# The adding DMAs read their second operand from SBUF, and the fills are put into a new order

## What is computed

```python
def swiglu_ffn(x, w_gate_up, w_down):
    g, u = jnp.split(x @ w_gate_up, 2, axis=-1)
    return (jax.nn.silu(g) * u) @ w_down

for layer in range(DEPTH):                       # DEPTH = 2, D_FF = 2816
    x = x + 0.5 * swiglu_ffn(rms_norm(x, ffn1_norm[layer]), ...)
    x = x + mixer(rms_norm(x, mix_norm[layer]))  # layer 0: windowed GQA, layer 1: latent attention
    x = x + 0.5 * swiglu_ffn(rms_norm(x, ffn2_norm[layer]), ...)
return rms_norm(x, final_norm)
```

## Time and profile before

| | us |
|---|---|
| runs (3) | 1857.53 median, 1855.23 to 1859.74 |
| profiled execution, its time | 1855.27 |
| profiled execution, span from first to last instruction | 1853.5 |
| PE busy in the span | 1737.3 |
| DVE busy | 1417.2 |
| ACT busy | 954.8 |
| POOL busy | 434.8 |
| mean granted TensorE clock | 0.981 |

### The profile page before, as it was taken

One profiled execution on the slowest core, in us unless ns is written; L12 is line 12 of the kernel. 1 busy time (PEld: TensorE's weight loads), 2 busy tenths in 40 slices (PEclk: granted clock), 3 DMA queues, 4 the chain that ended last, 5 costly groups with the idle time before them and its releaser, 6 DMA issues. The chain is left out here.

```text
span 1853.5 us, 34651 instructions
## 1 busy us (share of the span) xinstructions
PE 1737.3 (94%) x12937; PEld 1626.4 (88%) x12937; DVE 1417.2 (76%) x2776; ACT 954.8 (52%) x1892; POOL 434.8 (23%) x495
## 2 busy tenths in 40 slices
PE   5999999999989999999799999999999889999997
PEld 4999999877879899998799999987867789999995
DVE  5788787667678878866778788766897568878788
ACT  4554554446555545544555455544565445555452
POOL 0333333111013333330133333300000033333320
PEclk7999999999989999999899999999999989999999
DMA  5899999533439999995399999945112389999971
GB/s 173 192 219 237 224 220 229 149 110 91 125 91 220 221 228 217 226 245 154 69 224 224 226 223 230 209 117 132 30 40 58 108 182 220 230 226 221 226 163 69
DMA packets 187076, 324.18 MB, mean 175 GB/s; under 512 B 24545, under 2 KB 58526, under 8 KB 186910
## 3 DMA queue, kind: packets, MB, share of 16 engines
q0 software_dynamic: 66816, 121.66, 38.5%
q1 hardware_dynamic: 118528, 198.55, 33.9%
q10 hardware_dynamic: 1566, 1.74, 0.3%
HBM read 315.33 MB, written 2.10 MB: 171 GB/s over the span
## 5 line engine op out<-in xcount | busy, mean ns | idle before, releaser
L1889 PE MATMUL bank<-h_all,w_all 128*128 128x256 f32 x2352 | 672.2, 286 | 45.0 <-ACT work L1042 34.0
L1890 PE MATMUL bank<-h_all,w_all 128*128 128x256 f32 x2352 | 668.2, 284 | 0.0
L1891 PE MATMUL bank<-h_all,w_all 128*128 128x256 f32 x2352 | 668.0, 284 | 0.0
L1889 PEld LDWEIGHTS bank<-h_all,w_all 128*128 128x128 f32 x2352 | 453.9, 193 | 52.4 <-issue 34.4
L1890 PEld LDWEIGHTS bank<-h_all,w_all 128*128 128x128 f32 x2352 | 454.1, 193 | 0.0
L1891 PEld LDWEIGHTS bank<-h_all,w_all 128*128 128x128 f32 x2352 | 453.9, 193 | 0.0
L787 POOL DMA_DIRECT2D work<-ffn_gu x252 | 221.6, 923 | 825.3 <-DVE w_all L1238 593.3
L901 ACT ACTIVATE w_all<-work 128x512 fp32r<-128x512 f32 x352 | 208.9, 623 | 345.6 <-DMA work<-ffn_gu 222.3
L1238 DVE TENSOR_TENSOR w_all<-work,w_all 128x512 fp32r<-128x512 f32 x352 | 238.9, 687 | 150.4 <-ACT w_all L901 149.6
L1238 DVE TENSOR_TENSOR w_all<-r_all,w_all 128x512 fp32r<-128x512 f32 (+1 forms) x356 | 308.2, 866 | 21.7 <-ACT w_all L901 16.9
L901 ACT ACTIVATE w_all<-r_all 128x512 fp32r<-128x512 f32 (+1 forms) x356 | 273.0, 769 | 73.3 <-PE bank L1891 71.9
(11 more groups left out here) (214 smaller groups left out, 2787.1 us busy)
## 6 DMA issues: line engine op xcount, KB each, us to landing
work<-ffn_gu POOLq DMA_DIRECT2D x252, 256.0 KB, 5.9
r_all<-ffn_gu SPq DMA_DIRECT2D x88, 512.0 KB, 5.2
r_all<-ffn_gu SPq DMA_DIRECT2D x172, 256.0 KB, 6.3
work<-ffn_d POOLq DMA_DIRECT2D x96, 256.0 KB, 6.1
work<-ffn_gu SPq DMA_DIRECT2D x88, 256.0 KB, 5.6
r_all<-ffn_gu POOLq DMA_DIRECT2D x84, 256.0 KB, 7.2
r_all<-ffn_d SPq DMA_DIRECT2D x64, 256.0 KB, 5.8
r_all<-ffn_d SPq DMA_DIRECT2D x32, 512.0 KB, 5.3
```

The costliest lines, as they stand in the source:

```text
L1889: t.matmul(o, wh, xh, start=c == 0 and not on, stop=False, skip_group_check=on)
L1890: t.matmul(o, wh, xl, start=False, stop=False, skip_group_check=on)
L1891: last = t.matmul(o, wl, xh, start=False, stop=c == PAIRED - 1, skip_group_check=on)
```

## The change

Three things are changed together.

1. The addend of all adding DMAs (`link` and `join`) is the plain buffer of the unit in SBUF, not HBM. POOL therefore waits for the plain buffer's load before each, and SP waits, before it loads a plain buffer anew, for the third adding DMA of the unit that used it. In the last block the loads of `ffn_rows` wait for the adding DMAs of units 27, 28 and 29.
2. In a unit, FB(u) and FE(u) move from the end of iteration u-1 into iteration u: FB before FU(u+1), FE after the copy s_1. The addition of product 7 moves to the start of the next iteration on DVE (`finish`, `finish_late`). The third link of a unit is issued at the start of its own iteration.
3. At the start of a block: `pairs_out` evacuates a tile before it splits the next weights and fills FA(0), FU(0), FC(0) at j = 4, 5, 6 in place of 6, 7 and the end; FU(1) is filled at its end. In block 0 the combinations of the pairs move behind the sum of squares, and PE does `sums` after the second half of the plain tile and `spread` after product 2.

```diff
     def fill_count(f, kind, u):
-        at = {FA: 0, FU: 1, FC: 2}[kind] if u == 0 else {FU: 3, FA: 4, FB: 5, FE: 6, FC: 9, FD: 11}[kind]
-    elif u == NU - 1 and kind in (FC, FD):
-        at = 6 * NU - (5 if kind == FC else 4)
+        at = {FA: 0, FU: 1, FC: 2}[kind] if u == 0 else {FU: 3, FA: 4, FB: 5, FE: 6, FC: 9, FD: 10}[kind]
+    elif kind in (FU, FA):
+        at = (7 if kind == FU else 8) if u == 2 else 6 * u - (6 if kind == FU else 4)
     else:
-        at = 6 * u + {FU: -5, FA: -4, FB: -2, FE: 0, FC: 3, FD: 5}[kind]
+        at = 6 * u - 1 + {FB: 0, FE: 2, FC: 4, FD: 5}[kind]
...
     def load_plain(f, u):
-                if u >= 3:
-                    sp.wait_ge(fill_lo, fill_count(f, FC, u - 3))
-                elif f > 0:
-                    sp.wait_ge(fill_lo, fill_count(f - 1, FC, u - 3 + NU))
+                if u >= 3 or f > 0:
+                    fe, ue = (f, u - 3) if u >= 3 else (f - 1, u - 3 + NU)
+                    sp.wait_ge(fill_lo, fill_count(fe, FC, ue))
+                    if ue > 0:
+                        sp.wait_ge(chain_sum[(NU * fe + ue) % CHAIN], chain_count(fe, ue, 3))
...
     def load(n, src):
                 if n >= N_LAST and i < SLOTS:
+                    for u in (NU - 3, NU - 2, NU - 1):
+                        sp.wait_ge(chain_sum[(NU * f + u) % CHAIN], chain_count(f, u, 3))
...
     def link(f, u, step):
-                pool.dma_start(chain[g % CHAIN], unit_source(f, u, slice(part * S, (part + 1) * S)), accum_op=ALU.add
+                pool.wait_ge(plain_in[(u + 2) % 3], unit_count(f, u))
+                pool.dma_start(chain[g % CHAIN], plain[(u + 2) % 3][:, part * S:(part + 1) * S], accum_op=ALU.add
...
     def ffn(f, m):                                  # POOL
                 link(f, 1, 0)
                 join(f, 1)
-                for u in range(NU + 1):
+                for u in range(NU):
+                    if u > 0:
+                        link(f, u, 2)
                     link(f, u + 1, 1)
                     if u == 0:
                         power(m)
                     link(f, u + 2, 0)
                     join(f, u + 2)
-                    link(f, u + 1, 2)
...
     def pairs_out(n, f, begun=0):                   # ACT; DVE alike
+                if not begun:
+                    high(n + AHEAD, end)
                 for j in range(KD):
-                    if j >= begun:
-                        high(n + j + AHEAD, end)
-                    if j == KD - 2:
-                        high_fill(f, FA, 0)
-                    if j == KD - 1:
-                        high_fill(f, FU, 0)
+                    high(n + j + AHEAD + 1, end)
+                    if 4 <= j < 7:
+                        high_fill(f, (FA, FU, FC)[j - 4], 0)
+                    if j >= 2 and j % 2 == 0:
+                        high_mixed(h_mix, combine_count(f, j // 2 - 1, False), j // 2 - 1)
...
     def ffn(f):                                     # ACT
+                    if u > 1:
+                        high_fill(f, FB, u)
                     high_fill(f, FU, u + 1)
...
+                    if u > 1:
+                        high_fill(f, FE, u)
                     high_fill(f, FA, u + 1)
...
-                    high_fill(f, FB, u + 1)
+                    if before:
+                        silu(f, u - 1, 1)
                     high_fill(f, FD, u)
...
-                    high_fill(f, FE, u + 1)
...
     def ffn(f, m):                                  # DVE
+                    if u > 1:
+                        finish(f, u - 1)
+                        low_fill(f, FB, u)
                     low_fill(f, FU, u + 1)
+                    if u > 1 and UNITS[u - 1][0] == "D":
+                        finish_late(f, u - 1)
...
     def ffn(f, m, ready):                           # PE
                 plain_tile(f, False)
-                sums(m, KD)
+                if f > 0:
+                    sums(m, KD)
                 plain_tile(f, True)
                 if f > 0:
                     pe.wait_ge(evac_done, ready)
+                else:
+                    sums(m, KD)
                 product(f, 1, 1)
-                spread(m + 1)
-                for q in (2, 6, 5, 7):
+                if f > 0:
+                    spread(m + 1)
+                product(f, 2, 1)
+                if f == 0:
+                    spread(m + 1)
+                for q in (6, 5, 7):
                     product(f, q, 1)
```

More of the change, by code:

```diff
@@ L794, in join @@
                 pool.wait_ge(single_in[u % SINGLE], single_count(f, u))
-                pool.dma_start(single[u % SINGLE], unit_source(f, u, slice(0, S)), accum_op=ALU.add
+                pool.wait_ge(plain_in[(u + 2) % 3], unit_count(f, u))
+                pool.dma_start(single[u % SINGLE], plain[(u + 2) % 3][:, 0:S], accum_op=ALU.add
                                ).then_inc(single_sum[u % SINGLE], 16)
@@ L970, in pairs_out @@
                     squared(xT[:, PERM[j], :], j == 0)
-                    if j % 2 == 0 and j >= 2:
-                        high_mixed(h_mix, combine_count(f, j // 2 - 1, False), j // 2 - 1)
-                high_fill(f, FC, 0)
+                high_fill(f, FU, 1)
             def begin(f):
-                high_fill(f, FU, 1)
+                if f == 0:
+                    high_fill(f, FU, 1)
+                    high_fill(f, FA, 1)
+                    for q in range(PAIRED - 1):
+                        high_mixed(h_mix, combine_count(f, q, False), q)
                 high_mixed(h_mix, combine_count(f, PAIRED - 1, False), PAIRED - 1)
-                high_fill(f, FA, 1)
+                if f > 0:
+                    high_fill(f, FA, 1)
                 high_fill(f, FB, 1)
@@ L1077, in _ @@
                 squared(xT[:, PERM[j], :], j == 0)
-                if j % 2 and j < KD - 1:
-                    high_mixed(h_mix, combine_count(0, j // 2, False), j // 2)
             end = SEG_AT[1]
@@ L1342, in pairs_out @@
                 end = n + KD
+                if not begun:
+                    low(n + AHEAD, end)
                 for j in range(KD):
-                    if j >= begun:
-                        low(n + j + AHEAD, end)
-                    if j == KD - 2:
-                        low_fill(f, FA, 0)
-                    if j == KD - 1:
-                        low_fill(f, FU, 0)
                     b = product(n + j)
@@ L1463, in second_half, with finish, finish_late @@
                 v.tensor_tensor(hid_half(UNITS[u][1], 1), c_22[u % 2], g_1, ALU.mult).then_inc(late_half, 1)
+            def finish(f, u):
+                dve.wait_ge(prod_done, product_count(f, 7, u))
+                if UNITS[u][0] == "G":
+                    dve.wait_ge(e_7, order_of(f, u) + 1)
+                    dve.wait_ge(late_half, TILES * f + max(UNITS[u][1] - 1, 1))
+                    v.tensor_tensor(c_22[u % 2], C_BANKS[u % 2][:, 0:HN], u_3, ALU.add).then_inc(e_5, 1)
+                else:
+                    x_added(UNITS[u][2] + PAIRED, 1, B_BANKS[u % 2][:, 0:HN]).then_inc(e_7, 1)
+            def finish_late(f, u):
+                dve.wait_ge(e_7, order_of(f, u) + 1)
+                x_added(UNITS[u][2] + PAIRED, 1, C_BANKS[u % 2][:, 0:HN]).then_inc(e_5, 1)
             def ffn(f, m):
@@ L1496, in ffn @@
                         x_added(c0, 0, D_BANK[:, 0:HN]).then_inc(e_2, 1)
+                    if u > 1:
+                        low_fill(f, FE, u)
                     low_fill(f, FA, u + 1)
@@ L1536, in ffn @@
                         low(SEG_AT[f] + 1, end)
-                    if gate:
-                        dve.wait_ge(e_7, at + 1)
-                        dve.wait_ge(prod_done, product_count(f, 7, u))
-                        dve.wait_ge(late_half, TILES * f + max(UNITS[u][1] - 1, 1))
-                        v.tensor_tensor(c_22[u % 2], c, u_3, ALU.add).then_inc(e_5, 1)
-                    else:
-                        dve.wait_ge(prod_done, product_count(f, 7, u))
-                        x_added(c1, 1, b).then_inc(e_7, 1)
                     if q is not None:
                         low_mixed(y_mix, k, q % PAIRED)
-                    low_fill(f, FE, u + 1)
-                    if not gate:
-                        dve.wait_ge(e_7, at + 1)
-                        x_added(c1, 1, c).then_inc(e_5, 1)
                     if f == FFNS - 1 and u > DOWN_END[1]:
```

49 lines of the change are left out of this document (30 added, 19 removed).

## The result

The changed kernel takes 1842.12 us (median of 7 runs, 1840.71 to 1847.77) where the kernel before took 1857.53 (7 runs): a ratio of 0.9924, 95% interval 0.9908 to 0.9939, or 15.4 us less. The forecast was 1829.5, 28 us less.

The account below looks back on a forecast made before the run. PE was busy 1737.3 of 1853.5 us, with DVE and the DMA engines near it. Gains of 19 + 5 + 3 + 11 + 5 less losses of 8 and 7 made 28, so a median of 1829.5 us, range 1800 to 1877.

Parts of the forecast that it names:

- two serial reads stay two serial reads: Adding DMAs: taking the addend from SBUF changes nothing in a packet's cost; bounds 0 to 2.2 us a unit.
- rival (c): Adding DMAs with SBUF addends land 1 us or more sooner than 5.9, no ring misses: 1809 us; chance 0.20.
- 19 + 5 - 8 = 16 us: Units: 19 gained at waits for u_3, 5 where D units begin, 8 lost to small misses of the ring.
- the new order takes FB(u+1) from in front of u_3: Combining units: FB's landing gets 3 to 4 us more; 28 us of u_3 waits can go, 19 counted.
- The ring of the plain buffers: Units: link 2, plain load, link 0, FU, link 1, FB take 27.9 of 30.1 us; 8 us lost, bounds 0 to 56.
- 8 waits of 1.42: Where D units begin: PE's waits shrink to 0.8, as low_mixed is drawn forward and FE goes behind; 5 us gained.
- Block 0 was to start product 6(1) at about 51: Start of block 0: DVE's reordered work reaches about 51 before product 6(1) can start; 3 us gained, not 14.65.
- the four starts: Block starts: 3 us from block 0, 0 and 1.5 from blocks 1 and 3, 6 from block 2, 3 from FU(1); 14 together.
- The clock: After PE waits, as at the start of block 1: half of some 10 us of low-clock loss goes, 5 us gained.
- the wait for link 2: End of block 3: ffn_rows loads wait for unit 29's link 2, delaying product 7 by 6.5; 7 us lost with transposes.
- rival (a): Units: waits mostly move; ring misses and DVE lateness take 0.3 us in each of 112 units: 1855 us; chance 0.14.
- the signs that were named: Profile after: u_3 below 18 us, four units 41 or less, adding share near 38%, block 3 wait 5 to 8, acc wait split.

Follow-up runs that it names:

- order_only: Changed kernel with addends read from HBM again and without the waits the SBUF source brought, leaving parts 2 and 3: 1881.37 us, 1.0104 of the kernel before.
- hbm_waits: Changed kernel with its order and new waits kept, but all addends read from HBM again: 1886.68 us, 1.015 of the kernel before.
- fu_behind: Changed kernel with FU(u+1) filled behind the copy s_1 and its addition, on ACT and DVE: 1849.23 us, 0.9944 of the kernel before.
- starts_old: Changed kernel with part 3, the new block starts, taken back on ACT, DVE and PE: 1857.31 us, 0.999 of the kernel before.
- ends_fixed: Changed kernel with SP's table loads behind four down-weight loads and ffn_rows loads waiting only for units whose buffers they overwrite: 1821.31 us, 0.9792 of the kernel before.
- fb_behind_u3: Kernel before plus parts 1 and 3 and the mended ends, with FB(u+1) filled behind copy u_3 and product 7's addition: 1807.11 us, 0.9714 of the kernel before.
- source_only: Kernel before with only part 1, addends from SBUF and the waits that brings: 1843.21 us, 0.9905 of the kernel before.

## Why the prediction came out as it did

**The source of the addend: the step that failed.** The prediction says of it "I take nothing: two serial reads stay two serial reads". The price of a packet did stay, at 0.171 us. But a DMA's price for the engines and its time to land are two things. The landings fell from 5.9 to 5.2 us for the links, and part 1 alone, source and waits together, was worth 16 us. The rival (c) had the right place. Its step of 1 us or more came for the first link in the old order (1.6) and for no other, where it had it for all, on top of an order that was to bring 19 by itself. The Trainium skill's HBM Reference, section Latency, has 2 us for an access at high load; 0.7 us is what the links' landings show in the old order, 0.3 to 0.6 with order and waits equal. By the two rates of the Trainium skill's DMA: Bandwidth & Descriptors, section Where 436 GB/s comes from, the source would not matter; by the packets it didn't, by the time it did.

**The new order: right by the sum, wrong by the cause.** Units were to gain 19 + 5 - 8 = 16 us and gained 16.1. That the two agree is luck: with the old source the same order loses 20.7 there, and with the new source the old order gains 17.7. In the step "the new order takes FB(u+1) from in front of u_3" I followed what FB left and not what it came to stand ahead of. FB at the head of an iteration puts FU(u+1), and with it a landing, in front of s_1 a moment later: ACT stood 13 us for FU's landing in all (units 4 to 28) in the kernel before, 50 in the changed one, 89 in `order_only`. And link 2 goes out behind FB, at 3.3 us into its iteration (median; 1.1 before) where I had 1.7. So the order as a whole gained at product 4 only as far as landings came sooner (30.0 us lost before, 12.2 changed, 27.0 in `order_only`), and lost at product 6 (17.1, 20.7, 34.9). The ring of the plain buffers, priced at 8 us and feared at 56, is not in these losses: `hbm_waits` and `order_only` differ by 2.3 us in the units.

**The D groups.** 8 waits of 1.42 were to shrink to 0.8. Product 6 of the first D units lost 13.0 us before and 11.1 after, 1.39 a time, so 2 us came of the 5. Only `fu_behind` brought it to 0.78.

**The starts held.** Block 0 was to start product 6(1) at about 51; it started at 50.45, behind a wait that is now in two:

```profile
40.21 0.65 PE L2008 MATMUL bank<-ident,st 128*128 128x128 f32 x4 [2.25 <-DVE st L1329]
50.45 0.57 PE L1916 MATMUL bank<-h_all,w_all 128*128 128x256 f32 x1 [9.58 <-DVE w_all L1250]
```

14 us were counted for the four starts, 5.5 + 7.5 = 13.0 measured, and `starts_old` gives 12 to 15. The parts lay otherwise: block 0 gained 5.5 for 3, block 2 7.4, block 3 2.9, and block 1 lost 2.8. Its stage holds the low clock behind the end of block 0, and in `ends_fixed`, without that, it is 2.0 us shorter than before.

**The clock: a term that didn't come.** 5 us were counted. The mean granted clock of the profiled execution is 0.98 where it was 0.981, and at the start of block 1 it is low as before (0.50 from 540 to 545 us, 0.51 in the earlier trace rows). The new low stretches at the ends of blocks 0 and 3 took what others gave back. With the ends mended it is 0.987.

**The ends: one term right, one missing.** For block 3 the wait for link 2 was priced at 7; between `order_only` and the changed kernel it is 24.5 - 18.1 = 6.4. What was missing is that FE(29) moved too and that SP has a load behind it. The prediction followed the new waits past each queue and not the moved fills: with FE in iteration 29, the table and the down weights behind it go 3.4 us later. The ends of blocks 0 and 2 are 4.8 and 3.3 us longer. Another 4.2 at block 3 come with the order alone (18.1 for 13.9). DVE turns the result in pairs of transposes, 2.50 us a pair, at the ends of the last iterations. In the kernel before, FB(29) and the addition of product 7(29) came ahead of such a pair; in `order_only` each comes behind one. Product 6(29) starts 5.9 us into the unit for 4.3, and product 3(29) stands 1.89 us for the addition:

```profile
1821.06 2.50 DVE L1420 STREAM_TRANSPOSE x_f<-xT 32x1024 f32<-32x1024 f32 x2
1823.60 0.42 DVE L1487 TENSOR_TENSOR work<-bank,work 128x256 f32<-128x256 f32 x1
```

```profile
1824.17 0.55 PE L1911 MATMUL bank<-h_all,w_all 128*128 128x256 f32 x1 [1.89 <-DVE work L1487]
```

These 12 us are the larger part of the 15 by which the forecast missed the span; the 5 for the clock are missing too, against 2.5 gained in the tail. The measured 1842.1 lies as near to rival (a), 1855, as to the forecast, 1829.5, but not by (a)'s cause: the units lost nothing against the sum, the ends and the clock did.

**Of the signs that were named,** u_3 below 18 us (14.2), a share near 38% (38.7) and the wait of block 0 in two came. Four units were to take 41 us or less; the same four (from product 4(5) to 4(9) of block 2) took 41.89:

```profile
sum 41.89, PE 41.27 PEld 40.52 DVE 36.60 ACT 24.39 POOL 13.99; mean PE 41.27 PEld 40.52 DVE 36.60 ACT 24.39 POOL 13.99
```

and in `fb_behind_u3` 40.75. The wait at the end of block 3 came as 4.96 and 2.18. The sign against, ACT standing for landings before FU, showed in 37 of 100 units: that was the one to have weighed more.

## What to carry to other kernels

When a step is moved in an in-order queue, list what it now stands ahead of as carefully as what it leaves, on every engine that counts on its semaphore; the two misses here (FU ahead of s_1, FE(29) ahead of SP's load) are the same omission. Price a DMA twice, by what it takes of the engines and by when it lands, because where consumers wait in order the second is what counts. And when several changes come together, run each alone: here the units' sum was right while the part that was to bring it cost 16 to 18 us inside the whole, and the smallest piece of that part, with the rest left out, was worth 10.

## What the runs showed of the hardware

An adding DMA of 256 KB costs the DMA engines about the same with its addend in SBUF as in HBM (0.171 us a packet before and in the changed kernel; 0.167 in `source_only`), and lands sooner: 0.7 us as the median of the links in `source_only`, where the new waits came with it, and 0.3 to 0.6 between `hbm_waits` and the changed kernel, where only the source differs. SP's single loads of 256 KB land sooner too, though they were left as they were: 5.8 us for 6.3 in `source_only`, 5.8 for 6.7 against `hbm_waits`. Yet putting back 30.4 MB of the reads cost at most 2 to 3 us for the joins or for link 2, and 16 to 20 for link 0: what a read from HBM costs was here a matter of who waits for it. A wait of PE of 3.83 us was followed within a microsecond by a granted clock of 0.50, for some 10 us; with waits of 1.47 and 1.68 us at that place, and of 0.72, the clock stayed at 1.00.
